# Memory keys made between the modulation's slabs, and the first block's last norm applied behind the next block's products

## The reference, cut to what matters

```python
# first block
mod = silu(c) @ ada_w + ada_b                    # 1024 x 3072: shift, scale, gate
h = rms_norm(x, norm_g) * (1 + scale) + shift
p = h @ w_in                                     # then an RWKV-7 branch and a sparse attention branch
x = x + gate * (merged @ w_o)
x = rms_norm(x, final_g)                         # the first block's last norm
# second block
h = rmsnorm(x, ffn1_pre_g)
x = x + 0.5 * rmsnorm(swiglu(h, ffn1_w_in, ffn1_w_down), ffn1_post_g)
# ... HGRN2 and Fox branches, joined by gates, w_out, rmsnorm(.., mix_post_g) ...
h = rmsnorm(x, mem_pre_g)
mem_n = rmsnorm(mem, mem_kv_g)                   # mem: 256 x 1024, an input
q = h @ w_mq
k, v = split(mem_n @ w_mkv)                      # 1024 x 2048: the keys are the first 1024 columns
x = x + rmsnorm(softmax(q k^T / 16) v @ w_mo, mem_post_g)
x = x + 0.5 * rmsnorm(swiglu(rmsnorm(x, ffn2_pre_g), ffn2_w_in, ffn2_w_down), ffn2_post_g)
```

## Time and profile before

| | |
|---|---|
| median of 3 runs | 1289.8 us |
| profiled execution, its own time | 1291.93 us |
| its span on the core | 1290.1 us |
| TensorE busy | 1180.9 us (92%) |
| GpSimd busy | 905.7 us (70%) |
| ScalarE busy | 593.4 us (46%) |
| VectorE busy | 467.7 us (36%) |
| bytes read | 194.31 MB, 151 GB/s over the span |

### The profile page before, as it was taken

The page is one execution under the profiler, slowest core; times in us unless marked ns, Lnnn a source line. Parts: engine busy times, 40 slices in busy tenths (PEclk is TensorE's granted clock), DMA queues, the critical chain, the costliest instruction groups (busy, mean ns, idle before and its releaser), DMA issues.

```text
span 1290.1 us, 21180 instructions
## 1 busy us (share of the span) xinstructions
PE 1180.9 (92%) x8372; PEld 997.0 (77%) x8372; DVE 467.7 (36%) x833; ACT 593.4 (46%) x869; POOL 905.7 (70%) x913
## 2 busy tenths in 40 slices
PE   2998999999898999998999888989889999999997
PEld 2898987776677888787978867777669877888785
DVE  6476436744443111004246565331333133111101
ACT  2464133236435454435444346644465444544533
POOL 0688434434495888885999985679779756888784
PEclk9999799999999999999999999999899999999999
DMA  9656223333454666554655443436546534666562
GB/s 334 195 146 172 62 67 101 114 99 99 161 166 148 182 192 180 179 182 113 184 145 147 134 145 100 147 104 191 174 135 183 162 98 147 182 185 187 164 197 97
DMA packets 182915, 196.76 MB, mean 153 GB/s; under 512 B 7416, under 2 KB 141856, under 8 KB 182688
## 3 DMA queue, kind: packets, MB, share of 16 engines
q1 hardware_dynamic: 178336, 186.62, 48.2%
q10 hardware_dynamic: 4480, 8.78, 2.1%
HBM read 194.31 MB, written 1.06 MB: 151 GB/s over the span
## 4 chain that ended last, share of the span: by engine, by line
PE 72%; POOL 9%; DVE 8%; issue 5%; ACT 5%; DMA 2%; POOLq 0%; ACTq 0%; SPq 0%; DVEq 0%
PE ps L633 20%; PE ps L635 19%; PE ps L634 19%; PE ps L630 11%; POOL wlo L2493 9%; PE ps L638 3%; DMA raw<-in_ada_w 1%; ACT whi L1225 1%; DVE hE L1746 1%; DVE gt L1746 1%; ACT L1225 1%; DVE x L1754 1%; DVE acc L1754 0%; DVE gab L1746 0%; ACT gt L1225 0%
## 5 line engine op out<-in xcount | busy, mean ns | idle before, releaser
L2493 POOL TENSOR_TENSOR wlo<-raw,whi 128x256 fp32r<-128x256 f32 (+1 forms) x904 | 900.2, 1028 | 369.2 <-ACT whi L1225 365.4
L1225 ACT ACTIVATE whi<-raw 128x1024 fp32r<-128x1024 f32 x325 | 341.4, 1056 | 317.6 <-PE ps L635 296.8
L633 PE MATMUL ps<-whi,hThi 128*128 128x512 f32 (+2 forms) x672 | 269.4, 401 | 10.8 <-POOL wlo L2493 5.2
L635 PE MATMUL ps<-whi,hTlo 128*128 128x512 f32 (+2 forms) x672 | 260.6, 388 | 0.0
L634 PE MATMUL ps<-wlo,hThi 128*128 128x512 f32 (+2 forms) x672 | 260.0, 387 | 0.0
L633 PE MATMUL ps<-hThi,whi 128*128 128x256 f32 x576 | 171.1, 297 | 11.5 <-issue 4.6
L634 PE MATMUL ps<-hTlo,whi 128*128 128x256 f32 x576 | 164.7, 286 | 0.0
L635 PE MATMUL ps<-hThi,wlo 128*128 128x256 f32 x576 | 164.5, 286 | 0.0
L633 PEld LDWEIGHTS ps<-whi,hThi 128*128 128x128 f32 x672 | 128.1, 191 | 40.5 <-issue 13.3
L635 PEld LDWEIGHTS ps<-whi,hTlo 128*128 128x128 f32 x672 | 128.3, 191 | 26.7
L634 PEld LDWEIGHTS ps<-wlo,hThi 128*128 128x128 f32 x672 | 128.5, 191 | 21.9
(11 more groups left out here) (364 smaller groups left out, 1542.1 us busy)
## 6 DMA issues: line engine op xcount, KB each, us to landing
raw<-in_w_in SPq DMA_DIRECT2D x121, 512.0 KB, 3.6
raw<-in_ffn_w_in SPq DMA_DIRECT2D x176, 256.0 KB, 3.1
raw<-in_ffn_w_down SPq DMA_DIRECT2D x44, 512.0 KB, 3.6
raw<-in_ada_w SPq DMA_DIRECT2D x24, 512.0 KB, 5.3
raw<-in_w_mkv SPq DMA_DIRECT2D x16, 512.0 KB, 3.7
raw<-in_w_o SPq DMA_DIRECT2D x8, 512.0 KB, 3.6
raw<-in_w_branch_a SPq DMA_DIRECT2D x8, 512.0 KB, 3.7
raw<-in_w_branch_b SPq DMA_DIRECT2D x8, 512.0 KB, 3.7
```

What stands on the lines that cost most here:

```text
L633: e.matmul(o, l[0], r[0], start=start, stop=False)
L635: return e.matmul(o, l[1], r[0], start=False, stop=stop)
L1225: return e.activation(o, i, f, **k)
L2493: p = e.tensor_tensor(wlo[c % NHL][:, o], raw[i % NRAW][:, o], whi[c % NHL][:, o], ALU.subtract)
```

## The change

What it does:

- The memory is loaded first of all, into a part of `gab`; it is normed and turned around at the start (`key_norm`, tiles `mThi` and `mTlo`). The 8 slabs of keys are loaded between and behind the modulation's slabs, five of them between, and their products run there (`key`), with the planner's look-ahead of slabs down to 2 for the first four. The keys are kept in `qabs` and, since this tile is needed for the first block, written to device memory (1 MB, `key_store`); they come back to `kb` before the attention (`mem_load`). The normed memory itself is written out too (2 MB, `m_store`, started from ScalarE's queue) and read back for the values (`memx_load`).
- Of the 16 modulation slabs VectorE sums 8 as before; the other 8 are multiplied by `silu(c)` on TensorE, straight from the raw buffer (`mod_part`, 16 matmuls of 64 weight columns with one moving column for each slab). `keep_busy` is gone there. `x` is loaded in front of the eleventh slab, and most of the constants (now 0.94 MB) behind the start.
- At the seam `x` is turned around as it is; `hThi` and `hTlo` are scaled by `fpg`, the product of both gains. The first block's root and the scaling of `x` come after the four pairs, in `ffn_norm`; the FFN's products are scaled by the product of both roots. The first three slabs of each FFN are split by GpSimd in 4 pieces and no longer in one.
- The chain `memnorm` is gone. `mixend` now has the values' first half ("mv0", 4 slabs) and 10 matmuls on nothing beside it, `memlog` the second half.

```diff
+NA = CON["flip"][0]
 class Plan:
-        for n in range(4):
-            for kh in range(4):
...
-                do("ada", 4 * n + kh)
...
-        do("busy", 12, "main")
+        def key(c, i=None):
+            self.unit("fm", key_slab(c) if i is None else i, f"mk{c // 2}", "key", c // 2 * 2, "m", 0,
+                      j=c % 2, last=c % 2 == 1, ahead=2 if c < 4 else 3)
+        for i in range(8):
+            if i >= 3:
+                key(i - 3, early if i == 3 else None)
+            modulate(i)
+            modulate(i + 8)
+            if i == 0:
+                early = key_slab(0)
+                do("keynorm")
+            if i == 4:
+                do("load", "m_store")
+            if i == 6:
                 do("xnorm")
+        do("mod")
         do("hfirst")
+        for c in range(5, 8):
+            key(c)
         do("load", "small")
...
         do("busy", 24)
-        do("xfinal")
         do("load", "f1")
...
-        do("start", "memnorm")
+        do("load", "memx")
...
-        do("finish", "memnorm")
         do("start", "mixend")
-        for j in range(4):
-            fm(f"mk{j}", rows["w_mkv_2"], 256 * j, 256, "copy", ("kb", 2 * j), "oa", 2)
+        tm("mv0", rows["w_mkv_2"], [(1024, 512)], "tmcopy", ("vb", 0), "oa", 2)
+        do("busy", 10)
         do("finish", "mixend")
...
-        for n in range(2):
-            tm(f"mv{n}", rows["w_mkv_2"], [(1024 + 512 * n, 512)], "tmcopy", ("vb", n), "oa", 2)
+        tm("mv1", rows["w_mkv_2"], [(1536, 512)], "tmcopy", ("vb", 1), "oa", 2)
 tensor:
+            def mod_part(s):
+                i = plan.ada[s]
+                n, kh = divmod(s, 4)
+                w.wait_ge(S["ada"], "cs")
+                w.wait_ge(S["raw", i % NRAW], i)
...
+                for k in range(2):
+                    kk = 2 * kh + k
+                    for q in range(4):
+                        for p0 in (0, 64):
+                            m = mm(PS[7][p0:p0 + 64, 4 * n + q:4 * n + q + 1], r[:, k, q * 128 + p0:q * 128 + p0 + 64],
+                                   cs[:, kk:kk + 1], False, (s, k, q) == (15, 1, 3))
+                m.then_inc(S["mm"].tick(("use", i), ("mod", s)), 1)
             def ffn_norm(tag):
-                norm_turn("ffnnorm" + tag, x, *[("post_v", ({"1": "x", "2": "mem"}[tag], t)) for t in range(2)])
+                norm_turn("ffnnorm" + tag, x, *[{"1": ("ev_v", ("sum", "x", 1, t)), "2": ("post_v", ("mem", t))}[tag]
+                                                for t in range(2)])
 scalar:
             def ffn_norm(tag):
+                for t in range(2 if tag == "1" else 0):
+                    r = st[:, 2 + t:3 + t]
+                    act(FF[tag]["yg"][:, t, :], x[:, t, :], ACT.Square, accum_out=r).then_inc(S["post_a"].tick(), 1)
+                    w.wait_ge(S["post_a"])
+                    act(r, r, ACT.Sqrt, scale=1.0 / 1024, bias=C("eps", 0, 1)).then_inc(S["post_a"].tick(("x", t)), 1)
                 for t in range(2):
                     rstd(name, x, t, FF[tag]["yg"][:, t, :], [("post_v", ({"1": "x", "2": "mem"}[tag], t))])
+            def m_store():
+                w.wait_ge(S["lhs"], ("m", 0, 7, 1))
+                for z, d in zip(mT, m_dram):
+                    e.dma_start(d, z[:, :, :].rearrange("p f t -> p (f t)").bitcast(F32)).then_inc(S["m_out"].tick("out", by=16), 16)
 vector:
             def ffn_norm(tag):
+                if tag == "1":
+                    x_final()
                 for t in range(2):
                     recip_of(name, t)
+                    if tag == "1":
+                        w.wait_ge(S["norm_v"])
+                        tt(st[:, t:t + 1], st[:, t:t + 1], st[:, 2 + t:3 + t], ALU.mult).then_inc(
 gpsimd:
+            for tag in "12":
+                whole -= {first_slab[f"f{tag}0"] + k for k in range(NHL)}
```

More of the change, by code:

```diff
@@ L28 @@
 CON = {}
-for _n, _w in [("ident", 128), ("flip", 128), ("strict", 128), ("incl", 128), ("zero", 128), ("causal", 128),
-               ("ones64", 128), ("four", 1), ("off", 7 * 128), ("pair", 5 * 64), ("eye", 64), ("low", 5 * 16), ("eye32", 32), ("reset", 256), ("one", 256),
-               ("eps", 4), ("hot", 384)]:
+for _n, _w in [("ident", 128), ("eps", 4), ("flip", 128), ("strict", 128), ("incl", 128), ("zero", 128), ("causal", 128),
+               ("ones64", 128), ("four", 1), ("off", 64), ("pair", 5 * 64), ("eye", 64), ("low", 5 * 16), ("eye32", 32), ("reset", 256), ("one", 256),
+               ("hot", 384)]:
     CON[_n] = (sum(w for _, w in CON.values()), _w)
@@ L49, in constants @@
     put("ones64", s // 64 == t // 64)
-    put("off", np.concatenate([(s // (2 << l) == t // (2 << l)) & ((s >> l) % 2 == 0) & ((t >> l) % 2 == 1)
-                               for l in range(7)], axis=1))
     col = np.arange(64)[None, :]
+    put("off", (s % 64 // 2 == col // 2) & (s % 2 == 0) & (col % 2 == 1))
     put("pair", np.concatenate([(s % 64 // (2 << l) == col // (2 << l)) & ((s >> l) % 2 == 1) & ((col >> l) % 2 == 0)
@@ L234, in build @@
             fm(g, w, c0, n, "shift", f0)
+            if g == "k0":
+                do("load", "key_store")
         do("start", "bias")
@@ L553, in vcol, with gcol @@
             return vec[:, o:o + w]
+        def gcol(name, j):
+            return fpg[:, j:j + 1] if name == "ffn1_pre_g_2" else vcol(name, j)
         def tmv(key):
@@ L605, in sync @@
                     if slabs[old][2]:
-                        w.wait_ge(S["ada" if old < 16 else "mm"], ("use", old))
+                        w.wait_ge(S["ada" if old in summed else "mm"], ("use", old))
                     else:
@@ L617, in sync @@
             w.wait_ge(S["bias_out"], "out")
+            w.wait_ge(S["m_out"], "out")
+            w.wait_ge(S["k_out"], "out")
         def tensor(e):
@@ L1200, in tensor @@
                     next(chains[d[0]])
-                elif what == "ada" and d[0] > 9:
-                    w.wait_ge(S["ada"], ("use", d[0]))
-                    keep_busy(5, "main")
+                elif what == "ada" and d[0] >= 8:
+                    mod_part(*d)
+                elif what == "ada" and d[0] == 7:
+                    mod_sum()
+                elif what == "keynorm":
+                    norm_turn("key", gtm[:, :, 1024:2048], ("norm_a", ("key", "x", 1)), ("norm_v", ("key", "x", 1)))
                 elif what == "busy":
                     keep_busy(*d)
-                elif what == "mod":
-                    mod_sum(d[0])
                 elif what == "xnorm":
+                    turn["side"][0] += 1
                     w.wait_ge(S["const"], "first")
@@ L1381, in unit @@
                 if half == 0 and u.kind != "gate":
-                    round_slabs(place[u.slab] + NHL)
+                    round_slabs(place[u.slab] + u.ahead)
                 if u.kind == "tail" or (u.kind == "down" and u.last):
@@ L1702, in scalar @@
                     post(*d)
+                elif what == "keynorm":
+                    key_norm()
                 elif what == "xnorm":
@@ L2455, in vector @@
                     next(chains[d[0]])
-                elif what == "ada":
+                elif what == "ada" and d[0] < 8:
                     ada(*d)
-                elif what == "mod" and d[0] == 1:
-                    modulation()
                 elif what == "turn":
@@ L2515, in gpsimd @@
                     if d[1] == 0 and d[0].kind != "gate":
-                        remainders(place[d[0].slab] + NHL)
-                elif what == "hfirst":
-                    remainders(NHL)
+                        remainders(place[d[0].slab] + d[0].ahead)
+                elif what == "keynorm":
+                    remainders(1)
                 elif what == "step":
```

173 lines of the change are left out of this document (101 added, 72 removed).

## The result

| | before | after |
|---|---|---|
| median, runs on one chip | 1288.5 us (4 runs, 1286.4 to 1291.6) | 1306.5 us (4 runs, 1305.4 to 1312.6) |
| profiled execution, its span | 1291.9, 1290.1 us | 1306.7, 1304.5 us |
| `hsc` | 40.3 us | 72.1 us |
| first eviction of `w_in` | 54.2 us | 91.6 us |

The account below looks back on a forecast made before the run. TensorE, busy for 1180.9 of 1290.1 us, was taken as the bound. Start +28.4, memory attention -26.4 and seam +1.8 gave a span of 1293.9 us; the median forecast was 1294, range 1277 to 1303.

Parts of the forecast that it names:

- The memory attention: Memory stage: 20.4 saved on keys, 6.5 on the memory's norm, 0.5 lost on the second turn of weights; -26.4 us.
- rival D: Memory stage saves only 20 us, since `x`'s norm isn't hidden by four slabs: 1300 us; chance 0.12.
- The seam: Between the blocks: the turn of `x` comes 1.4 us earlier, but the FFN's fourth slab comes late; +1.8 us.
- The start: Up to the first `w_in` product: the chain of loads, sums and keys puts `hsc` at 66 us; +28.4 us.
- rival C: In the start: products between waits run at a lower clock, +8 us at most, +5 taken: 1299 us; chance 0.15.
- The store: In the start: 2 MB of normed memory goes out beside key 3's load; that product at 52 us, 49.2 without it.
- Behind `hsc`: End of the start: the first `w_in` slab's product ends 13.7 us behind `hsc`, at 79.7 us.
- Rival B: In the start: loads keep ahead, `hsc` at 50 us, start 12 us late and not 28: 1277 to 1278; chance 0.28.

Follow-up runs that it names:

- filled: The changed kernel with matmuls on nothing in TensorE's gaps of the start; ratio to before 1.0076, `hsc` at 68.7 us.
- ring5: The changed kernel with five raw buffers for slabs and not four; ratio to before 1.0098, `hsc` at 68.3 us.
- store_late: The changed kernel with the 2 MB of normed memory stored behind the last key, not behind key 1; ratio to before 1.0219.
- queued2: keys_queued with the memory's low halves behind VectorE's sixth sum, not its first, and the 2 MB store behind the first `w_in` products; ratio to before 1.0128.
- queued8: The changed kernel, all keys behind the modulation's slabs, queues reordered, five raw buffers, matmuls on nothing before key 0 and the turn of `x`; ratio to before 1.0001.
- seam_alone: The kernel before with only the new seam and the first three slabs of each FFN in 4 pieces; ratio to before 1.0039.
- seam_round: seam_alone with the FFN's fourth slab rounded by ScalarE between the two norms' squares and roots; ratio to before 1.0026.
- keys_queued: The changed kernel with all 16 modulation slabs loaded first and all 8 slabs of keys behind them; ratio to before 1.0141.

## Why the prediction was wrong, point by point

- **The memory attention, -26.4:** measured -25.9. The split is a little off. From the last copy behind `w_out` (below) to the first queries out it took 1024.96 - 999.77 = 25.2, before 1000.02 - 967.57 = 32.5, so 7.3 saved where the sum has 26.7 - 17.7 = 9.0. The norm of `x` is hidden, as forecast: its turn follows the 10 matmuls on nothing without a wait. What the sum lacks are two waits for the subtractions of the values' slabs, 0.91 and 1.04, whose roundings stand between the steps of this norm on ScalarE. The stretch behind the queries gives 10.7, for 10.9. The rest, 7.9 ahead of that copy, was put at 6.5, for the memory's norm. So rival D's reason did not come true; 1.7 of its 6.4 us were lost all the same, for another one, and nearly paid back. TensorE has 19.0 us from the copy to the first query product, where I gave 17:

```profile
999.77 0.69 DVE L1822 TENSOR_TENSOR gt<-ps,row 128x512 f32<-128x512 f32 x1 [0.69 <-PE ps L671]
...
1006.22 0.47 PE L669 MATMUL ps<-whi,oahi 128*128 128x512 f32 x1 [0.91 <-POOL wlo L2586]
1010.25 0.47 PE L669 MATMUL ps<-whi,oahi 128*128 128x512 f32 x1 [1.04 <-POOL wlo L2586]
...
1015.32 1.91 PE L674 MATMUL ps<-con,gt 128*128 128x128 f32 x16
1018.77 0.36 PE L669 MATMUL ps<-hThi,whi 128*128 128x256 f32 x1 [1.54 <-DVE hTlo L1830]
```

- **The seam, +1.8:** the mechanism was right, to the number: the fourth slab was rounded at 442.4 and subtracted by 446.0, where my 410.4 plus the 35.4 us of lateness is 445.8. I gave no price to the clock behind the wait (nine matmuls at 0.43 us and not 0.23, 1.8 in all), and so the stage cost 3.4 at the second gate.
- **The start, +28.4: this is the step that failed.** It came to +37.3, and of the 8.9 between them 6.1 are lost up to `hsc`, which was to come at 66 and came at 72.1. The waits were followed in the right order, and the queue was right to the eighth load (out at 22.1, for 21.9) and key 1's slab (23.7, for 23.5). What failed is a price: each product stands in the sum with 2.84 us, from a stage in which TensorE never waits. The keys between waits took 4.3, 5.4 and 4.9 (keys 1 to 3), key 4 behind the turn took 4.1, and the turn of `x` 3.65 for 1.9. On the chain stand keys 1, 3 and 4 and the turn (key 4 starts 3.3 us behind it): 1.5 + 2.1 + 1.2 + 1.4 = 6.2 us more than I had. The other misses nearly cancel: key 1's slab landed 1.3 late, in 6.0 us, and the load of key 3's slab followed key 1's product by 3.2 and not 2.5; against that `mod_part`, which no row could price, took 1.1 and not 2.0 at the chain's end (1.9 in two of its eight places), the steps between key 3 and the turn took 0.6 less, and the terms gave 65.5, which I wrote as 66. Key 3's landing, 7.6, is near what the sum has for it with the store, 5.0 + 2.8.

  I had the clock as rival C, gave it 0.15, and priced it at 5 us beside the sum and not in it. Run filled takes 3.4 of it back at `hsc`; key 1's slab landed 1.3 us later in that execution, which is as much as its product gained. The Trainium skill ("TensorE: Matmul & The Clock Gate", section "HAM oscillation") had warned of just this shape of work; the trace agrees, 0.50 in three of the four windows above.

  Run ring5 shows that the transfers hold this stage too. The DMA engines were nearly full from 28 to 44 us (1.09 and 0.96 in the windows above), and a fifth buffer, which lets the loads start earlier, is worth 3.8; but this is no term that was mis-sized, for the sum had four buffers in it. With clock and ring both mended `hsc` is at 65.3.
- **The store:** taken at two thirds of 4.2 us on the chain, 2.8; store_late gives 2.3 at key 3's landing. In store_late and queued2 the same transfer costs TensorE's time beside `w_in`, where I had put transfers at nothing. The rule of the Trainium skill that I weighed ("DMA: Bandwidth & Descriptors", section "Issuing engines are not separate DMA queues") holds in its direction: 7.6 us with the store out, 5.3 without it.
- **Behind `hsc`:** 19.5 us to the first eviction, where the sum gives 54.2 + 28.4 - 66 = 16.6. That is the rest of the 8.9, and the same price again. TensorE stopped for 3.6 us in front of key 7, and its product then took 4.3 us, with a granted clock of 0.62 from 80 to 84 us, for the 2.84 of the sum; it started 1.1 later than the +8.1 that I had for its subtraction's end. ring5, with the same order, has 17.6: there the clock was at 1.00 from 76 us on and key 7 took 3.1.

```profile
81.30 0.55 PE L669 MATMUL ps<-mThi,whi 128*128 128x256 f32 x1 [3.58 <-POOL wlo L2586]
```

- **Rival B** (a start filled well, faster) was the idea's own case. `hsc` at 40.1 was reached in queued8, with all keys behind it, and even that ends at no change that can be told. To fill TensorE's idle time with keys means 5 MB more of loads in a stage in which the DMA engines are nearly full.

## What to carry to other kernels

A product that stands between two waits is priced at the clock of a stretch that also stands between waits, not at that of the full stages: put the clock in the sum, not beside it. Before work is moved into an idle stretch of one engine, look at what that stretch is full of: here the DMA engines, one in-order queue and four buffers. And a transfer costed at nothing needs a window of the place where it will run, not the mean over the span (151 GB/s here, against 383 in that window).

## What the runs showed of the hardware that was not expected

**The time of an execution goes with its mean granted clock.** Of the 17 executions of the kernel before in the last comparison, the fastest was 1287.1 us at a clock of 0.985 and the slowest 1300.7 at 0.974; a straight line through all 17 has 10.7 us less for each 0.01 more. One stretch of the second block, with the same work, was granted full clock in the profile of before and not in that of seam_alone, which comes to it 4.0 us later. TensorE alone, in before, then in seam_alone:

```profile
780.00:800.00 20.00, 17.54 (x103) 1.00 0.36 107
```

```profile
784.00:804.00 20.00, 17.60 (x82) 0.83 0.27 79
```

From behind the seam to 893 us the lateness of seam_alone grows from 3.8 to 10.5 us, and that of seam_round from -0.2 to 6.8, with no change in the work between; at the end 8.2 and 4.7 are left. It may be that an edit that moves work in time changes what the clock does far behind it, and that this is the 0.26% of seam_round. Neither is shown: each kernel has one profile, and executions of one and the same kernel differ by as much.

**TensorE also runs at half its rate where the granted clock reads 1.00.** In keys_queued all 24 products of the first key and the first ones of the second took 0.64 us for each three, from 54.5 to 60.4 us, and the others 0.36 from 60.9 on, in windows that read 1.00:

```profile
48.00:56.00 8.00, 6.40 (x49) 1.00 0.74 195
56.00:60.00 4.00, 4.00 (x21) 1.00 0.76 223
```

In the kernel before, the 16 matmuls at 22.43 took 3.54 us and the same at 38.21 took 1.84, both where the clock reads 1.00. So the column alone does not show it; the duration of a known product does.
